# Second modulation layer's sums on GpSimd, and four weight parts per norm with tile 1 behind tile 0

## The reference

```python
def ada_modulation(c, ada_w, ada_b):            # c [1, 1024], ada_w [1024, 6144]
    m = jax.nn.silu(c) @ ada_w + ada_b
    return jnp.split(m, 6, axis=-1)
def modulate(h, shift, scale):
    return h * (1.0 + scale[:, None, :]) + shift[:, None, :]
def swiglu(h, w_gate, w_up, w_down):
    return (jax.nn.silu(h @ w_gate) * (h @ w_up)) @ w_down
def odd_layer(x, c, ...):                       # even_layer has another mixer, the rest is alike
    sh_m, sc_m, g_m, sh_f, sc_f, g_f = ada_modulation(c, ada_w, ada_b)
    h = modulate(rms_norm_2(x, mix_norm), sh_m, sc_m)
    ...                                         # qkv, stick-breaking attention -> o
    x = x + g_m[:, None, :] * (o @ w_out)
    hf = modulate(rms_norm_2(x, ffn_norm), sh_f, sc_f)
    return x + g_f[:, None, :] * swiglu(hf, ffn_w_gate, ffn_w_up, ffn_w_down)
```

## Time and profile before

| what | value |
|---|---|
| median of 3 runs | 891.24 us (891.03 to 891.61) |
| the profiled execution: time, span | 891.4 us, 889.3 us |
| PE busy | 880.2 us, 99% of the span |
| DVE busy | 694.1 us, 78% |
| ACT busy | 501.6 us, 56% |
| POOL busy | 29.0 us, 3% |
| granted PE clock | full in all 40 slices |

### The profile page before, as it was taken

The page is one execution under the profiler, slowest core; times in us unless marked ns, Lnnn a source line. Parts: engine busy times, 40 slices in busy tenths (PEclk is TensorE's granted clock), DMA queues, the critical chain, the costliest instruction groups (busy, mean ns, idle before and its releaser), DMA issues.

```text
span 889.3 us, 13261 instructions
## 1 busy us (share of the span) xinstructions
PE 880.2 (99%) x4833; PEld 747.9 (84%) x4833; DVE 694.1 (78%) x735; ACT 501.6 (56%) x673; POOL 29.0 (3%) x52
## 2 busy tenths in 40 slices
PE   8999999999999999999999999999999999999998
PEld 5998878888888799979888888878777888888886
DVE  4698977988888987896888888687797875655655
ACT  5545665565555658756554455465675565545542
POOL 4000110000000100002000000010000000000000
PEclk9999999999999999999999999999999999999999
DMA  6989585899899384565988887536434366556551
GB/s 215 338 270 341 183 302 183 319 364 369 328 332 340 129 284 145 175 202 183 364 310 316 321 313 281 195 114 211 135 118 142 118 208 195 190 189 188 189 192 67
DMA packets 117091, 208.04 MB, mean 234 GB/s; under 512 B 7236, under 2 KB 81068, under 8 KB 111928
## 3 DMA queue, kind: packets, MB, share of 16 engines
q1 hardware_dynamic: 116566, 205.31, 67.1%
q10 hardware_dynamic: 290, 2.10, 0.7%
q0 software_dynamic: 192, 0.05, 0.0%
HBM read 206.39 MB, written 1.05 MB: 233 GB/s over the span
## 4 chain that ended last, share of the span: by engine, by line
PE 93%; DVE 4%; DMA 2%; issue 1%; ACT 1%; SPq 0%; DVEq 0%; ACTq 0%
PE ub L1937 11%; PE tp L1937 10%; PE acc L1837 7%; PE acc L1838 7%; PE acc L1840 7%; PE ub L1939 5%; PE acc L1800 5%; PE tp L1939 5%; PE acc L1802 5%; PE acc L1801 5%; PE tp L1957 4%; PE acc L1957 3%; PE acc L1923 3%; PE acc L1925 3%; PE acc L1924 3%; PE ub L2183 1%
## 5 line engine op out<-in xcount | busy, mean ns | idle before, releaser
L1157 DVE TENSOR_TENSOR w_lo<-w_raw,w_hi 128x1024 fp32r<-128x1024 f32 x283 | 341.8, 1222 | 105.1 <-ACT w_hi L728 104.7
L728 ACT ACTIVATE w_hi<-w_raw 128x1024 fp32r<-128x1024 f32 x283 | 296.8, 1057 | 211.9 <-PE acc L1840 49.8
L1937 PE MATMUL tp<-aT,w_hi 128*128 128x512 f32 x432 | 135.9, 396 | 0.0
L1937 PE MATMUL ub<-aT,w_hi 128*128 128x512 f32 x432 | 135.4, 395 | 0.0
L1837 PE MATMUL acc<-w_hi,hT_hi 128*128 128x512 f32 x284 | 110.8, 390 | 0.8 <-DVE w_lo L1157 0.8
L1838 PE MATMUL acc<-w_lo,hT_hi 128*128 128x512 f32 x284 | 110.6, 389 | 0.0
L1840 PE MATMUL acc<-w_hi,hT_lo 128*128 128x512 f32 x272 | 105.8, 389 | 0.0
L1939 PEld LDWEIGHTS tp<-aT,w_lo 128*128 128x128 f32 x432 | 81.2, 188 | 19.2
L1939 PEld LDWEIGHTS ub<-aT,w_lo 128*128 128x128 f32 x432 | 81.1, 188 | 18.9
L1939 PE MATMUL tp<-aT,w_lo 128*128 128x256 f32 x432 | 84.9, 278 | 0.0
L1939 PE MATMUL ub<-aT,w_lo 128*128 128x256 f32 x432 | 84.9, 278 | 0.0
(11 more groups left out here) (324 smaller groups left out, 1307.9 us busy)
## 6 DMA issues: line engine op xcount, KB each, us to landing
ada_raw<-in_l_ada_w SPq DMA_DIRECT2D x24, 1024.0 KB, 6.7
w_raw<-in_l_ffn_w_gate SPq DMA_DIRECT2D x44, 512.0 KB, 4.7
w_raw<-in_l_ffn_w_up SPq DMA_DIRECT2D x44, 512.0 KB, 3.8
w_raw<-in_l_ffn_w_down SPq DMA_DIRECT2D x44, 512.0 KB, 3.4
w_raw<-in_w_up SPq DMA_DIRECT2D x32, 512.0 KB, 4.8
w_raw<-in_w_down SPq DMA_DIRECT2D x32, 512.0 KB, 5.4
scratch<-in_l_ada_w SPq DMA_DIRECT2D x14, 1024.0 KB, 7.4
w_raw<-in_attn_w_qkv SPq DMA_DIRECT2D x24, 512.0 KB, 6.3
```

The costliest lines, as they stand in the source:

```text
L728: act.activation(rounded_part(v), w_raw[:, v % SLOTS, :], ACT.Copy).then_inc(hi_done, 1)
L1157: dve.tensor_tensor(rest_part(v), w_raw[:, v % SLOTS, :], rounded_part(v).bitcast(F32), ALU.subtract).then_inc(lo_done, 1)
L1937: pe.matmul(banks[f], rounded_part(v)[:, c[f]], aT[:, :, b, :], start=b == 0, stop=False)
```

## The change

**The sums.** The ten products with ones and the two pairs of rounded products of the second layer leave PE, and with them their ACT copies, the rounding step `K0` of `STICK_STEPS` and the table `ADA_ORDER`. POOL does the sums in their place by `partition_all_reduce`, twelve calls of 128x512, four behind each third. DVE now accumulates the second third in the first four of the eight rounds of the first gated feed-forward and the last third in the other four, both in `scratch` (`ada_acc`).

**The parts.** At each of the three places four whole weight parts get a home of their own in `scratch` (`hold`), and PE does all of tile 0 of them before any of tile 1. Some of these homes are where `ada_acc` is, so ACT waits for POOL's sums before it writes the last two in place B.

**The norms.** The two variants of the gated norm become one, squares are taken in halves of 512 columns, and POOL adds the halves.

```diff
@@ class of tiles and slots
+        with nc.sbuf_tensor("below_hold", [P, UNIT], F32), nc.sbuf_tensor("hold", [P, 8, PART], F32R) as hold:
+            pass
+        ada_acc = [scratch[:, n * UNIT:(n + 1) * UNIT] for n in (1, 2)]
...
+        held = {2 * u + n: homes[n] for u, homes in ((U_WOUT0 + 2, (3, 2, 1, 0)), (U_QKV2 - 2, (3, 2, 0, 1)),
+                                                     (U_WOUT1 + 2, (0, 1, 3, 2))) for n in range(4)}
+        apart.update({v: (hold[:, 2 * n, :], hold[:, 2 * n + 1, :]) for v, n in held.items()})
@@ POOL
+            def rstd_halves():
+
+                for t in range(NT):
+                    n_half[0] += 1
+                    n_rstd[0] += 1
+                    pool.wait_ge(sq_half, n_half[0])
+                    chained(pool.tensor_scalar(var[:, t:t + 1], half_sums[:, 2 * t:2 * t + 1], EPS, None, ALU.add))
+                    pool.wait_ge(sq_done, n_rstd[0])
+                    chained(pool.tensor_tensor(var[:, t:t + 1], half_sums[:, 2 * t + 1:2 * t + 2], var[:, t:t + 1], ALU.add))
+                    pool.tensor_tensor(rstd[:, t:t + 1], var[:, t:t + 1], half[:, 0:1], ALU.pow).then_inc(rstd_done, 1)
+
+            def partition_sums(dst, src):
+
+                for n in range(UNIT // CH):
+                    c = slice(n * CH, (n + 1) * CH)
+                    pool.partition_all_reduce(dst[:, c], src[:, c], P, bass.bass_isa.ReduceOp.add).then_inc(pool_sum, 1)
...
-            row_rstd()
+            rstd_halves()
             pool.wait_ge(xn_done, 16)
-            start_sums(1, 1)
-            start_sums(1, 2)
-            row_rstd()
+            start_sums(1, 1, ada_acc[0])
+            start_sums(1, 2, ada_acc[1])
+            pool.wait_ge(ada_used, 24)
+            partition_sums(mod[:, 0:UNIT], mod_next)
+            pool.wait_ge(ada_used, 32)
+            partition_sums(mod[:, UNIT:2 * UNIT], ada_acc[0])
+            pool.wait_ge(ada_used, 40)
+            partition_sums(mod[:, 2 * UNIT:3 * UNIT], ada_acc[1])
+            rstd_halves()
@@ ACT
+            def home_free(v):
+
+                if v < U_SG0 * 2:
+                    act.wait_ge(lru_ya if held[v] == 0 else lru_yb, 1)
+                elif v < U_QKV2 * 2:
+                    act.wait_ge(w_used, parts_to(U_SG0))
+                    if held[v] < 2:
+                        act.wait_ge(pool_sum, 8 + 4 * held[v])
+                elif held[v] < 2:
+                    act.wait_ge(z_ready, HEADS)
+                else:
+                    act.wait_ge(wT_ready if held[v] == 3 else so_ready, HEADS)
@@ DVE
+            def gated_norm(n, first, half, u_end, g_mod, g, shift):
+
+                def scale(t, h):
+                    c = columns(h)
+                    return dve.tensor_tensor(xn[:, t, c], x[:, t, c], g[:, c], ALU.mult)
+
+                dve.wait_ge(*first)
+                gated(0, g_mod, 0).then_inc(x_half, 1)
+                split_part(2 * u_end)
                 dve.wait_ge(tile0_done, n + 1)
                 gated(0, g_mod, 1).then_inc(x_ready, 1)
                 dve.wait_ge(x_ready, 2 * n + 1)
                 norm_scale(0, g)
+                dve.wait_ge(*half)
+                gated(1, g_mod, 0).then_inc(x_half, 1)
                 norm_rows(0, g, shift)
+                split_part(2 * u_end + 1)
+                dve.wait_ge(x_half, 2 * n + 2)
+                scale(1, 0).then_inc(norm_scaled, 1)
                 norm_lo(0, 0)
                 norm_lo(0, 1)
+                dve.wait_ge(w_used, parts_to(u_end))
+                gated(1, g_mod, 1).then_inc(x_ready, 1)
+                dve.wait_ge(x_ready, 2 * n + 2)
+                scale(1, 1).then_inc(norm_scaled, 1)
+                dve.wait_ge(norm_scaled, 2 * n)
                 norm_rows(1, g, shift)
...
+                if layer == 0:
+                    ada_gain(1, 1, pool_sum, 4)
                 one(u + 3 * NJ_SG - 4, NJ_SG - 1)
-                split_lo(u + 3 * NJ_SG)
...
-            ada_gain(1, 4, 20)
+            ada_gain(1, 4, pool_sum, 12)
@@ PE
+            def down_last(u, h, lo_count):
+
+                parts = [(2 * u + k - 2, 2 * (1 - h) + k) for k in range(2)] + [(2 * u + k, 2 * h + k) for k in range(2)]
+                for v, _ in parts:
+                    part_ready(v)
+                for n in range(2):
+                    for v, k in parts[2:]:
+                        down_block(v, k, 0, n, False, False, lo=False)
+                    if n == 0:
+                        pe.wait_ge(hT_lo_done, lo_count)
+                    for v, k in parts[2:]:
+                        last = pe.matmul(acc[:, n, :], hT_lo[:, k, 0:P], rounded_part(v)[:, n * CH:(n + 1) * CH],
+                                         start=False, stop=v == parts[3][0])
+                    last.then_inc((half_done, tile0_done)[n], 1)
+                for n in range(2):
+                    for v, k in parts:
+                        last = down_block(v, k, 1, n, False, v == parts[3][0])
+                        if n == 1:
+                            last.then_inc(w_used, 1)
+                    if n == 0:
+                        last.then_inc(half_done, 1)
...
-            ada_sums(1, 4, 6)
...
-            entry(U_QKV2, (acc[:, 0, :], acc[:, 1, :]), third_sum, last_sum, ada_parts=18)
+            entry(U_QKV2, (acc[:, 0, :], acc[:, 1, :]), no_sums, no_sums)
```

279 lines of the change are left out of this document (99 added, 180 removed).

## The result

The changed kernel takes 896.92 us (median of 6 runs, 894.90 to 897.29) beside 891.57 us for the kernel before (6 runs, 891.03 to 893.02) on the same chip: ratio 1.0054, 95% interval 1.0044 to 1.0064, so 0.54% slower. That lies in the range of the prediction (888.0 to 897.0), at its upper edge, but the likeliest case, no change at 892.1, did not come: 5.35 us were lost, not 0.9. Its runs fall into two groups, two at 894.9 and four from 896.9 to 897.3; the profiled one (896.95 us, span 895.1) is of the second.

What follows compares the result with a forecast made beforehand. PE was taken as the bound, waiting on DVE's rows at three norms: 0.55 + 0.8 - 0.45 = +0.9 us, so 892.1 us on the median (chance 0.53, own range 890.6 to 893.6); overall range 888.0 to 897.0.

Steps and rivals of the forecast that it cites:

- place B: Norm behind the first feed-forward's last projection: PE newly waits 0.65 us for all four parts; tile 1's transposes +0.8 us.
- rival 2: POOL's sums too slow for ACT's rounding, from 4.5 us a sum; 894.9 us at 5.2 each; chance 0.22.
- The 9.5 us turn into waiting: PE work removed with the sums becomes PE waiting before tile 1's transposes, 2.2 to 2.8 us at each place.
- T1: Start of PE's transposes of tile 1 at each of the three norms, forecast at 400.84, 589.63 and 704.37.
- rival 1: PE's cover, not DVE, decides at the three norms: gain 2.0, 2.0 and 2.7 us, 884.5 us; chance 0.14.
- Places A and C: First and third of the three norms: tile 1's transposes 0.55 us later at the first, 0.45 us earlier at the third.
- x(1): Moment DVE starts the gate of tile 1's second half, 10.77 us after the first gate starts, without a gap.
- the path to T1: From tile 1's second gate through ACT's squares, POOL's addition and power, and DVE's rows to tile 1's transposes: 4.20 us.
- POOL's addition: New one-column addition on POOL before the power in each norm: 0.37 us, taken between 0.19 and 0.55.
- The sums on POOL: Four sums ahead of ACT's last rounding: hidden if under 4.5 us each; estimated 4.05 us, ends 0.45 and 6.3.
- Rival 3: POOL's code exchange delays the second norm's rstd; decides above 11 us, costs 3 us at 14, 895.1 us; chance 0.08.
- Rival 4: Each POOL sum goes through its 128 partitions in turn, 58 us a sum, 1419 us in all; chance 0.03.

Runs made afterwards that it cites:

- the early gate: Changed kernel with DVE's gate of tile 1's second half moved directly behind tile 0's rows: 892.34 us, ratio 1.0014.
- idle products: Changed kernel with unused 512-wide PE products ahead of tile 1's transposes: ten at the second place only, 896.90 us; 9, 10 and 8 at all three, 896.06 us.

## Why the prediction was wrong, and where it was right

**The number lies in the range by luck.** 896.92 us is 0.08 below the range's upper bound, and that part of the range was there for sums too slow for ACT (rival 2), which did not happen. By the prediction's own bounds (no change up to 893.0 us) the outcome is "slower", which had 0.37 against 0.51 for no change.

**"The 9.5 us turn into waiting": right.** The waits at T1 are 2.09, 2.26 and 1.74 us, each 0.4 to 0.5 below its forecast (arrivals at 398.3, 586.9 and 702.2 against T1 at 400.84, 589.63 and 704.37), and the kernel before without these sums gains 0.7 us. That DVE and not PE decides at the three places, the argument against rival 1, is shown by the early gate, which takes 1.1 to 1.2 us off each place by moving DVE's work alone.

**Places A and C, "+0.55" and "-0.45": right**, +0.50 and -0.27. **x(1) and the path to T1** likewise: in B DVE starts tile 1's second gate at 588.75, 10.77 us behind the first gate at 577.98, to the last digit as worked out, and T1 comes 4.06 us behind that, for 4.20. POOL's addition, put at 0.37, took 0.19 for tile 1 and 0.40 for tile 0.

**Place B, "0.65 us of waiting that was not there": nearly right for the order, wrong for the kernel.** Without the sums the wait is 0.56, and T1 of B comes 189.80 us after T1 of A, against 188.55 before: the order costs 1.25 us where 0.8 was forecast, and the 0.45 between them was not taken apart. With the sums the wait is 1.30, and PE has lost more before it.

**The step that failed is "The sums on POOL. They are hidden if they are quick enough."** They were quick enough: 3.7 us each in the last third, below the 4.5 us that ACT allowed, and they ended at 568.93, ahead of ACT's last rounding. But I had tested them against one deadline on ACT only and taken their price on DVE from a memset, which reads nothing. A sum holds a DVE instruction with two operands in SBUF that starts in its midst until it ends or nearly so, by up to 2.1 us, and DVE is what feeds PE with splits. The term for it stood at nothing; it measures 2.5 us at place B (2.66 less 0.16, by which the kernel without sums was ahead at place A already). The Trainium skill (GPSIMD Engine Reference, Specifications) names just this pair, DVE instructions with two SBUF inputs; I had cited it, but had let it stretch POOL's sums (rival 2), when the rows show that it also stretches DVE's splits. The Trainium skill (Trainium Architecture — The Big Picture, What this means for kernel authors) calls the shared port an exclusive lock and no split of bandwidth. The rows agree: a held instruction ends with the sum or up to 0.45 us before its end, a sum that starts under a running split takes longer (3.99 for 3.23 us), and an instruction with an operand in PSUM is not held at all.

**A term that was missing: the clock.** Turning PE's work into one wait of 2.26 us was costed at nothing. The granted clock fell behind it, and from B's T1 to C's start it took 1.92 us longer than before: 99.31 us, against 97.69 in the kernels with the early gate and in those with idle products, whose clock did not fall there, so 1.6 us for the clock. The sum of the terms is then 0.5 in A, 1.25 for B's order, 2.5 for the sums, 1.6 for the clock and 0.3 behind B's T1, less 0.3 in C and less the 0.28 by which the kernel was ahead at A: 5.6 us at C's T1, of the 5.8 by which the spans differ.

**Rival 3, the exchange of code: rightly left aside.** POOL began to load it at 406.5 and the first sum started at 412.14, 5.6 us; the first operation of the rstd, at 580.26, waited for ACT alone. **Rival 4** is out: a sum takes 3.3 to 4.1 us, not 58. **Rival 2** named the right side, with a time 2 us short (894.9), but by another way: ACT never waited for a sum.

**What stays open:** why the same sums cost the kernel before so little, why the low clock comes in some executions only, and the spread of the runs with idle products.

## What to carry to other kernels

Work that leaves the busiest engine is worth only what the engine behind it can deliver sooner: at each place look for the row that is awaited last, and put what it needs ahead of what nobody waits for yet. Work moved to GpSimd has to be priced on VectorE too, where it can hold an instruction that reads two operands from SBUF until it ends; start it where the next such instruction is not yet awaited, or beside instructions that read PSUM. Spacing it out alone gave little here. And before an item moves on an in-order engine, list who waits for the items behind it: one memset behind four sums cost 11 us.
